# Beginning the first unit of three projections on TensorE at the end of the stage ahead of each

## What is computed

```python
# feed-forward of a layer; w_down is 2816 x 1024
u = h @ w_up
u = up[:, :-2] * conv_w[0] + up[:, 1:-1] * conv_w[1] + up[:, 2:] * conv_w[2] + conv_b
a, b = jnp.split(u, 2, axis=-1)
return (jax.nn.silu(a) * b) @ w_down
...
# attention over the memory
q = (hx @ w_mq).reshape(B, S, MEM_HEADS, MEM_HEAD_DIM)
k, v = jnp.split(hm @ w_mkv, 2, axis=-1)
...
p = jax.nn.softmax(s, axis=-1).astype(v.dtype)
o = jnp.einsum('bhsm,bmhd->bshd', p, v).reshape(B, S, MEM_HEADS * MEM_HEAD_DIM)
return o @ w_mo
```

## Time and profile before

| | |
|---|---|
| median of three runs | 2778.01 us (2770.65 to 2778.29) |
| profiled execution, time | 2779.62 us |
| profiled execution, span | 2777.8 us |
| TensorE busy | 2487.8 us (90%), 14602 matmuls |
| VectorE, ScalarE, GpSimd busy | 1375.2, 868.5, 251.7 us |
| mean granted TensorE clock | 0.949 of full |

### The profile page before, as it was taken

One profiled execution on the slowest core, in us unless ns is written; L12 is line 12 of the kernel. 1 busy time (PEld: TensorE's weight loads), 2 busy tenths in 40 slices (PEclk: granted clock), 3 DMA queues, 4 the chain that ended last, 5 costly groups with the idle time before them and its releaser, 6 DMA issues. The chain is left out here.

```text
span 2777.8 us, 34833 instructions
## 1 busy us (share of the span) xinstructions
PE 2487.8 (90%) x14602; PEld 1933.5 (70%) x14602; DVE 1375.2 (50%) x2185; ACT 868.5 (31%) x1385; POOL 251.7 (9%) x183
## 2 busy tenths in 40 slices
PE   7997988999998998997889999998977889898976
PEld 5885657888887787995669998764733368573322
DVE  4324554566667214325647777347565645423213
ACT  3222433332324113223444334233424642311001
POOL 0002520000000000003500000000042020011112
PEclk9998989999999999997989999999988999988999
DMA  5114731111111112115612223320201013348997
GB/s 240 61 54 106 269 128 46 46 61 61 63 69 38 53 63 82 61 69 142 224 46 92 92 92 117 111 82 31 87 0 54 0 61 137 121 188 326 421 421 292
DMA packets 58555, 326.88 MB, mean 118 GB/s; under 512 B 8157, under 2 KB 14429, under 8 KB 26461
## 3 DMA queue, kind: packets, MB, share of 16 engines
q1 hardware_dynamic: 45358, 302.76, 29.4%
q0 software_dynamic: 5696, 12.59, 1.2%
q10 hardware_dynamic: 7344, 9.28, 1.0%
HBM read 317.26 MB, written 12.58 MB: 119 GB/s over the span
## 5 line engine op out<-in xcount | busy, mean ns | idle before, releaser
L953 PE MATMUL ps<-work_rounded,ring_rounded 128*128 128x512 f32 (+1 forms) x2016 | 537.0, 354 | 19.1 <-DVE work_rounded L397 10.6
L953 PE MATMUL ps<-xn_rounded,ring_rounded 128*128 128x512 f32 (+2 forms) x2304 | 541.8, 347 | 0.0
L2003 PE MATMUL ps<-xn_rounded,ring_rounded 128*128 128x258 f32 (+2 forms) x2816 | 535.1, 312 | 0.0
L2003 PEld LDWEIGHTS ps<-xn_rounded,ring_rounded 128*128 128x128 f32 x2816 | 414.6, 191 | 31.2
L953 PEld LDWEIGHTS ps<-xn_rounded,ring_rounded 128*128 128x128 f32 x2304 | 373.4, 191 | 57.6 <-issue 0.2
L953 PEld LDWEIGHTS ps<-work_rounded,ring_rounded 128*128 128x128 f32 x2016 | 336.5, 192 | 76.3 <-DVE work_rounded L397 11.8
L953 PE MATMUL ps<-big_rounded,ring_rounded 128*128 128x512 f32 (+1 forms) x1200 | 326.3, 364 | 45.0 <-DVE big_rounded L859 25.0
L859 DVE TENSOR_TENSOR ring_rounded<-ring,ring_rounded 128x2048 fp32r<-128x2048 f32 (+2 forms) x94 | 189.1, 2015 | 266.5 <-ACT ring_rounded L824 266.5
L2003 PE MATMUL ps<-work_rounded,ring_rounded 128*128 128x256 f32 (+1 forms) x1232 | 280.2, 309 | 9.0 <-PEq L784 4.8
L953 PEld LDWEIGHTS ps<-big_rounded,ring_rounded 128*128 128x128 f32 x1200 | 203.4, 196 | 84.8 <-DVE ring_rounded L859 21.4
L824 ACT ACTIVATE ring_rounded<-ring 128x2048 fp32r<-128x2048 f32 (+2 forms) x94 | 158.2, 1687 | 314.7 <-PE ps L953 298.3
(11 more groups left out here) (420 smaller groups left out, 3125.4 us busy)
## 6 DMA issues: line engine op xcount, KB each, us to landing
ring<-in_stream SPq DMA_DIRECT2D x141, 1024.0 KB, 4.8
big<-in_experts SPq DMA_DIRECT2D x44, 1024.0 KB, 26.0
ring<-in_stream SPq DMA_DIRECT2D x32, 704.0 KB, 4.0
ring<-in_experts SPq DMA_DIRECT2D x22, 1024.0 KB, 27.3
xn<-in_experts SPq DMA_DIRECT2D x15, 1024.0 KB, 28.4
work<-in_experts SPq DMA_DIRECT2D x15, 1024.0 KB, 28.7
big<-in_first_modulation SPq DMA_DIRECT2D x8, 1024.0 KB, 14.1
work<-in_bias ACTq DMA_DIRECT2D x24, 256.0 KB, 3.9
```

The lines of the kernel that those rows point to most:

```text
L953: mm = pe.matmul(out[:, a - u.first:b - u.first], lhs, rhs, start=j == 0 and n == 0 and not u.onto, stop=j == terms - 1 and n == len(passe ...
L2003: mm = pe.matmul(out[:, a:b], ws[:, k, :], x[k][:, a - base:b - base], start=k == 0 and n == 0, stop=k == KT - 1 and n == 2)
```

## The change

At each of the three places matmuls of the next projection's first unit are issued by TensorE at the end of its list for the stage ahead, by a new function `begin_unit`, and `project` leaves them out (`begun`). No matmul, split or transfer is added or dropped. At C the begun matmuls belong to two units, and the splits of tiles 6 and 7 also move from the projection into the end of the attention.

```diff
+    def begin_unit(self, pe, out, strip, weight, sources):
+        slot = self.ring[:, strip % RING * STRIP:strip % RING * STRIP + WIDTH[strip]]
+        high_w, low_w = [self.rounded(self.high_of(strip))], [self.rounded(slot)]
+        for j, (low, high) in enumerate(sources):
+            for n, (w, x) in enumerate(((high_w, low), (high_w, high), (low_w, high))):
+                pe.matmul(out, weight(w, j), self.rounded(x), start=j == 0 and n == 0, stop=False)
...
     def project(...)
-                    for j, tile in enumerate(u.tiles):
+                    for j, tile in list(enumerate(u.tiles))[begun.get(i, 0):]:
...
+                if begin:
+                    begin(pe)
...
     def attention(...)
                 values(heads - 1)
+                if begin:
+                    pe.wait_ge(exped.sem, exped.at(units))
+                    begin(pe, 0)
...
+                if begin:
+                    begin(pe, 1)
...
                 store(heads - 1)
+                next_lows(units)
...
     def ffn_up(...)
+                if tiles_ahead:
+                    pe.wait_ge(next_low.sem, next_low.at(tiles_ahead + 1))
+                    self.begin_unit(pe, self.ps[:, 0:width], len(self.freed_at), self.down_weight, down_sources[0:tiles_ahead])
...
     def ffn_down(...)
-        self.project(units, 2 * KT, finish, banks_each=2, sources=sources, tiles_ahead=tiles_ahead,
+        self.project(units, 2 * KT, finish, banks_each=2, sources=sources, tiles_ahead=tiles_ahead, begun={0: tiles_ahead},
...
     def mixed_projection(self):
+        def begin(pe):
+            pe.wait_ge(strip_low.sem, strip_low.at(3))
+            pe.wait_ge(taken.sem, taken.at(1))
+            self.begin_unit(pe, self.bank(0, 256), memory_strip, halves(0), memory_norm.rooms[0:KT - 1])
...
     def memory_attention(self):
-        self.project(units, 12, finish, sources=norm.rooms, deferred=norm, early=KT, tiles_ahead=KT)
+        self.project(units, 12, finish, sources=norm.rooms, deferred=norm, early=KT, tiles_ahead=KT, begun={0: KT - 1})
...
+        def begin(pe, part):
+            if part == 0:
+                pe.wait_ge(next_low.sem, next_low.at(6))
+            self.begin_unit(pe, self.bank(2 * part), strip, halves(part), [(o[:, m, :], self.output_high[m]) for m in range(6)])
...
-            next_tiles=[(6 + 4 * (m // 2), 2 * (m // 2) + 2, o[:, m, :], self.output_high[m]) for m in range(6)])
+            next_tiles=[(6 + 4 * (m // 2) if m < 6 else 16, 2 * (m // 2) + 2, o[:, m, :], self.output_high[m]) for m in range(KT)], begin=begin)
...
-                               tiles_ahead=6, rooms=self.output_high)
+                               tiles_ahead=KT, rooms=self.output_high, begun={0: 6, 1: 6})
```

More of the change, by code:

```diff
@@ L878, in project @@
     def project(self, units, strips, finish, sources, banks_each=1, prefetch=None, deferred=None, add=None, gpsimd=None,
-                early=None, following_strip=False, loads=None, following_halves=False, after=None, beside=None, tiles_ahead=0):
+                early=None, following_strip=False, loads=None, following_halves=False, after=None, beside=None, tiles_ahead=0,
+                begun={}, begin=None):
         first = len(self.freed_at)
@@ L1169, in store, with next_lows @@
                         dve.tensor_copy(dst, opsum[m % len(opsum)][r0:r0 + rows, 0:nq * P]).then_inc(stored.up(), 1)
+                def next_lows(u):
+                    for n, (at_unit, _, value, high) in enumerate(next_tiles):
+                        if u == min(at_unit + 1, units):
+                            dve.wait_ge(next_high.sem, next_high.at(n + 1))
+                            self.split_low(dve, value, high).then_inc(next_low.up(), 1)
                 for u in range(3):
@@ L1180, in _ @@
                         self.low_ahead(dve, views)
[L1181 to L1184, removed]
+                    next_lows(u)
                 store(heads - 1)
+                next_lows(units)
                 if modulation:
@@ L1197, in exponentials, with next_highs @@
                                    accum_out=stat[:, 2, b:b + 1]).then_inc(exped.up(), 1)
+                def next_highs(u):
+                    for at_unit, outputs, value, high in next_tiles:
+                        if u == at_unit:
+                            act.wait_ge(stored.sem, stored.at(outputs))
+                            self.split_high(act, value, high).then_inc(next_high.up(), 1)
                 def square_pair(p):
@@ L1216, in _ @@
                         self.high_ahead(act, views)
[L1217 to L1220, removed]
+                    next_highs(u)
                     if pair_at(u, 2) is not None:
                         square_pair(pair_at(u, 2))
+                next_highs(units)
                 if normed_pairs:
@@ L1896, in _, with output_projection @@
                 normalise(2)
-    def output_projection(self, src, segments, residual, prefetch=None, add=None, gpsimd=None, next_sources=None, tiles_ahead=0, rooms=None):
+    def output_projection(self, src, segments, residual, prefetch=None, add=None, gpsimd=None, next_sources=None, tiles_ahead=0, rooms=None, begun={}):
         width = segments[-1][1]
@@ L1923, in output_projection @@
         self.project(units, 4, finish, banks_each=2, prefetch=prefetch, add=add, gpsimd=gpsimd, after=after,
-                     following_strip=bool(next_sources), following_halves=bool(next_sources), tiles_ahead=tiles_ahead,
+                     following_strip=bool(next_sources), following_halves=bool(next_sources), tiles_ahead=tiles_ahead, begun=begun,
                      sources=[(src(k)[:, 0:width], room) for k, room in zip(range(KT), rooms or tiles_in(width, self.work))])
@@ L2115, in ffn_down @@
         g, segments = self.g, self.gates(l, 5, need_ctx)
-        units = [Unit([2 * m, 2 * m + 1], lambda w, j: w[j // 11].rearrange("p (k c) -> p k c", k=FT // 2)[:, j % 11, :], range(FT), P, width)
-                 for m in range(KT)]
+        units = [Unit([2 * m, 2 * m + 1], self.down_weight, range(FT), P, width) for m in range(KT)]
         def finish(eng, i, ps):
```

16 lines of the change are left out of this document (10 added, 6 removed).

## The result

The changed kernel takes 2779.19 us (median of 20 runs, 2777.26 to 2784.61), the kernel before 2776.40 us on the same chip (median of 20, 2770.65 to 2780.28). The ratio is 1.0014, with a 95% interval of 1.0008 to 1.0020: the change costs a little, 2.2 to 5.6 us, and wins nothing.

A forecast was written before the change was run, and what follows sets the result against it. TensorE, busy 2487.8 of 2777.8 us, was taken as the bound. A +0.3 +2.4, B +0.7, C -0.6 sum to +2.8 us: 2782.4 on the profiled 2779.6, or 2780.8 us against the 2778.0 median; range 2773 to 2786.

The forecast's parts named there:

- two chains that begin at the barrier: Behind the ffn_up/ffn_down barrier and the mixed/memory projection one, ScalarE and VectorE work decides when TensorE can go on.
- A, barrier and chain, +0.3: ffn_up to ffn_down: begun matmuls end 0.66 us behind VectorE's gate, so tile 11 starts 0.3 us later.
- What decided before: ffn_down before the change: strip 1's readiness decides tile 11's start; 3.0 us of low clock beside the chain cost nothing.
- The wait: ffn_down's first unit: TensorE, through with tile 10 near 1727.9, idles 7.4 us until strip 1 is ready.
- A, clock, +2.4 (1.6 to 3.0): ffn_down behind the wait for strip 1: restart at low clock loses 2.4 us, taken from layer 0's same projection.
- B, chain, 0: Mixed to memory's projection: VectorE's chain to strip 2 keeps unit 4's start at 2304.15, so 0 us change.
- B, clock, +0.7 (0 to 1.4): Behind the wait for strip 2, grown from 2.84 to 6.9 us, the low clock costs 0.7 us more.
- C, -0.6: Attention's end to output projection: 36 begun matmuls hide VectorE's last copy, winning 0.6 us (0.3 to 0.9).
- The clock costs nothing more: Rival: TensorE leaves the new waits at full clock or pays only what it paid; 2777.7 us, chance 0.20.
- The holes are filled: Rival: no standing behind tile 10 and unit 3; 11.9 us won, 2766.1 us; chance 0.06 beyond 8.3 us.
- The begun units outlast the tail: Rival: low clock during ffn_down's 27 begun matmuls, chain 6.0 us late; +9.7 us, 2787.7 us, chance 0.05.

The follow-up runs named there:

- bc_only: Kernel before plus the change without the 27 begun ffn_down matmuls (only the 21 at B and 36 at C begun early): 2774.92 us, ratio 1.0001.
- a_alone: Kernel before plus only the 27 matmuls of ffn_down's first unit begun at the end of ffn_up: 2780.83 us, ratio 1.0014.
- a_warm: a_alone plus 24 additional unused matmuls between tiles 10 and 11 of ffn_down's first unit: 2775.27 us, ratio 0.9998 to the kernel before.
- defer_only: Kernel before with VectorE's inversion of the stream's root moved behind unit 6, nothing begun early: 2773.12 us, ratio 0.9991.
- a_early2: a_alone with strip 1 split ahead of tile 11, one more strip loaded first, filter features one unit later: 2774.73 us, ratio 0.9997 to the kernel before.
- b_defer: defer_only plus the 21 matmuls at B begun early: 2773.95 us, ratio 0.9990 to the kernel before.

## Why the prediction was right

The forecast was 2780.8 us and +2.8 on the profiled execution; measured were 2779.19 us, +2.8 between the medians, +3.9 by the ratio, +2.0 by the three places. That the medians give just +2.8 is luck. The direction and the mechanism were right: two chains that begin at the barrier, and the clock behind A's wait. The prediction took 8.3 us for the least that could be told from no change; the interval of twenty runs each, 2.2 to 5.6 us, does not hold zero. By its steps:

- **A, barrier and chain, +0.3: right, +0.16.** TensorE sets the barrier, by 0.50 us instead of 0.66, because the begun matmuls start (1712.40) 0.16 us ahead of the modelled end of `ffn_up`'s last four (1712.56); the wait for strip 1 came as described, 6.41 us where 7.4 were forecast.
- **What decided before was read a little too simply.** The text has strip 1 decide when tile 11 starts, and the 3.0 us of low clock cost nothing. But in the profile before TensorE had no wait ahead of tile 11: its own slow matmuls brought it there 0.36 us after the chain alone would have. With a low stretch of 6.8 us instead of 10.2 (`bc_only`) tile 11 started 0.37 us earlier. The sum has this in its 0.3, since it takes the 0.42 us into account.
- **The wait was sized wrong by 1 us.** The text had TensorE through with tile 10 near 1727.9, 1.3 us behind tile 9's split: six matmuls at full clock. In the profile after the clock fell while they ran, and they took 2.35 us (1720.50 to 1722.85, modelled end). It cost nothing, the chain being last.
- **A, clock, +2.4 (1.6 to 3.0): right.** 2.72 - 0.16 = +2.56 here, about +2.3 in `a_alone`, and with `a_warm` only 0.23 is left of both terms together. The price of the same projection in layer 0 came close; that is in part luck, since behind A's barrier the low stretch itself was 6.8 us long in one execution with this change and 13.7 in another.
- **B, chain, 0: right** (-0.04), and `defer_only` showed which instruction it hangs on.
- **B, clock, +0.7 (0 to 1.4): mis-sized, it is 0.** The clock was down 3.4 us behind the wait of 6.85 us, and 3.4 behind that of 2.84. I took the middle between two ends for a longer wait. The longer wait did make the low stretch longer, but by as much as it began earlier, inside the wait.
- **C, -0.6: right**, -0.68 and -0.71; the barrier that TensorE sets costs it 0.44 us.

The two mis-sized terms are of one sign (0.1 and 0.7 us too high) and small against the spread of the runs. The range of 2773 to 2786 is not quite what its terms give (2770.65 - 0.3 and 2779.62 + 4.4: 2770 to 2784). Of the rivals, "The clock costs nothing more" is refuted at A by `a_warm` and right at B. "The holes are filled" needs strip 1 early, which `a_early2` gave: even then the gain was 3.2 us and not 7.2, as shorter waits and the clock took half. "The begun units outlast the tail" did not come: the begun matmuls ran at 1.00.

## What to carry to other kernels

Before pulling ready matmuls over a barrier, look for what TensorE needs next behind them and when that chain starts: if the chain starts at the barrier, the idle time is only moved, and it may be moved from ahead of hidden work to ahead of work that TensorE bounds, where the half clock behind it is paid in full (here 2.2 to 2.6 us). Shorten the chain first (here one inversion moved, 4.6 us at B; one strip split earlier at A), and then begin only as much as doesn't bring TensorE to the next wait early. Compare such changes place by place with the same matmul in both traces, since the spans of two executions differ by more than the change.

## What the runs showed of the hardware

- **How long the clock stays low differs between executions of the same work.** Behind the barrier at A, with the same instructions around it, the low stretch was 10.2 us long in the profile before (1720.5 to 1730.7, the first 4.1 us of it idle) and 6.8 in those of `bc_only`, `b_defer` and `defer_only`. With the begun matmuls it was 6.8 us in that of `a_alone`, where it began late in the wait, and 13.7 in that of after, where it began during tiles 9 and 10 and lasted through the wait. The Trainium skill says as much for the start of a kernel (TensorE: Matmul & The Clock Gate, section "What's actually happening": the number of matmuls that run at the low clock varies from run to run), and these traces agree for a stretch in its middle. Stretches of before (it goes on in the earlier trace rows), of `bc_only` and of `a_alone`:

```profile
1720.50:1724.50 4.00, 0.00 (x0) 0.50 0.31 128
```

```profile
1720.70:1726.10 5.40, 5.38 (x13) 0.50 0.80 213
1726.10:1731.00 4.90, 4.90 (x23) 1.00 1.07 383
```

```profile
1729.40:1731.30 1.90, 0.00 (x0) 0.50 0.96 414
1731.30:1736.20 4.90, 4.90 (x12) 0.50 0.92 388
```

- **A busy TensorE can stay at the low clock.** 27.3 us at 0.50 without an idle moment, in two profiles. The same section has activity release the throttle; by that rule alone the stretch should have ended early, and here it didn't. The measurement decides: with these products, the clock does not always come back while they run.
- **Filler matmuls bring the clock back** at no cost where TensorE would wait: 24 of them, 6.59 us beside a wait of 6.41, were worth 2.2 us at A (+2.44 in `a_alone`, +0.23 with them).
